# Starting the differential-attention steps four ticks earlier in a single-core hybrid attention layer

## The reference

```python
proj = h @ w_in                     # h: (512, 1024), w_in: (1024, 11264)
qa, ka, va, za, qd, kd, vd, zd, gm = split(proj)
# 24 windowed heads in three groups (dilation 1, 4, 16), each with its softmax denominator
o_g, lse_g = dilated_window_attention(rope(qa), rope(ka), va, ...)
alpha = softmax(stack(lses), axis=0)
ya = sum(alpha[..., None] * stack(outs)) * silu(za);  pa = ya @ w_proj_a
# 8 differential heads, two softmaxes each
qd, kd = rope(qd), rope(kd)
p = softmax(q_c @ k_c.T * 64 ** -0.5)        # c = 0, 1
yd = rms_norm((p[0] - lam * p[1]) @ vd, diff_subln) * 0.8 * silu(zd);  pb = yd @ w_proj_b
ga, gb = split(sigmoid(gm))
y = rms_norm((ga * pa + gb * pb) @ w_out, norm_post);  out = x + gate * y
```

## Time and profile before

| | |
|---|---|
| median of 3 runs | 801.05 us |
| range of these runs | 800.49 to 1100.22 us |
| the profiled execution | 801.21 us |
| its span | 799.1 us |
| PE busy | 778.6 us, 97% of the span |
| PE weight load busy | 656.9 us, 82% |
| DVE, ACT, POOL busy | 420.2, 359.9, 452.4 us |
| mean granted TensorE clock | 0.992 of full speed |

### The profile page before, as it was taken

How to read it: one execution, slowest core, us unless ns; L and a number is a source line. 1 busy time by engine, 2 the same in 40 slices (tenths; PEclk the granted TensorE clock), 3 DMA queues, 4 the chain that set the end, 5 groups by cost and what they waited for, 6 DMA issues and landing times.

```text
span 799.1 us, 12588 instructions
## 1 busy us (share of the span) xinstructions
PE 778.6 (97%) x4590; PEld 656.9 (82%) x4590; DVE 420.2 (53%) x692; ACT 359.9 (45%) x777; POOL 452.4 (57%) x577
## 2 busy tenths in 40 slices
PE   4999999999999999999999999999999999999997
PEld 3787898888888888898797888888787878878997
DVE  4766664635455443344675576487557445324432
ACT  5555535545444444343464555455556333314311
POOL 7854545446656654369663696596454287837200
PEclk9799999999999999999999999999999999999999
DMA  9955323233343432352431433242212145615431
GB/s 317 348 168 155 86 84 104 81 98 115 107 119 105 121 107 80 107 151 81 140 97 54 121 105 121 78 123 76 82 34 74 35 151 213 208 53 177 139 106 53
DMA packets 87075, 95.38 MB, mean 119 GB/s; under 512 B 9405, under 2 KB 78310, under 8 KB 87014
## 3 DMA queue, kind: packets, MB, share of 16 engines
q1 hardware_dynamic: 86944, 94.56, 38.3%
q10 hardware_dynamic: 70, 0.02, 0.0%
HBM read 78.53 MB, written 5.54 MB: 105 GB/s over the span
## 4 chain that ended last, share of the span: by engine, by line
PE 90%; issue 3%; POOL 3%; DVE 1%; DMA 1%; ACT 1%; SPq 0%; DVEq 0%; POOLq 0%; ACTq 0%
PE proj L1747 64%; PE sums L1670 4%; PE proj L1867 4%; PE score L1586 4%; PE turned L1638 3%; PE score L1620 3%; PE proj L1796 2%; PE sums L1672 2%; POOL w_lo L819 1%; PE score L1608 1%; DMA x_in<-in_x 1%; PE score L1796 1%; PE turned L1680 0%; PE turned L1694 0%; POOL merged L796 0%
## 5 line engine op out<-in xcount | busy, mean ns | idle before, releaser
L819 POOL TENSOR_TENSOR w_lo<-raw,w_hi 128x256 fp32r<-128x256 f32 x376 | 299.9, 829 | 212.7 <-ACT w_hi L932 212.7
L1747 PE MATMUL proj<-h_hi,w_hi 128*128 128x512 f32 x560 | 229.4, 410 | 0.1
L1747 PE MATMUL proj<-h_hi,w_lo 128*128 128x512 f32 x560 | 219.3, 392 | 0.0
L1747 PE MATMUL proj<-h_lo,w_hi 128*128 128x512 f32 x560 | 218.7, 391 | 0.0
L1747 PEld LDWEIGHTS proj<-h_hi,w_hi 128*128 128x128 f32 x560 | 105.2, 188 | 30.4 <-issue 9.6
L1747 PEld LDWEIGHTS proj<-h_hi,w_lo 128*128 128x128 f32 x560 | 105.1, 188 | 23.2
L1747 PEld LDWEIGHTS proj<-h_lo,w_hi 128*128 128x128 f32 x560 | 105.5, 188 | 19.1 <-issue 0.5
L932 ACT ACTIVATE w_hi<-raw 128x1024 fp32r<-128x1024 f32 x96 | 100.4, 1054 | 15.7 <-PE proj L1747 11.2
L1380 DVE TENSOR_TENSOR at_lo<-turned,at_hi 128x512 fp32r<-128x512 f32 x64 | 44.1, 689 | 80.6 <-ACT at_hi L1070 80.0
L848 POOL TENSOR_TENSOR rope_x<-rope_x,cos_t 128x512 f32<-128x512 f32 x36 | 53.4, 1484 | 51.6 <-DMA rope_s<-rope_x 51.6
L1670 PE MATMUL sums<-v,at_hi 128*128 128x128 f32 (+1 forms) x256 | 60.8, 307 | 0.0
(11 more groups left out here) (291 smaller groups left out, 1479.7 us busy)
## 6 DMA issues: line engine op xcount, KB each, us to landing
raw<-in_w_in SPq DMA_DIRECT2D x85, 512.0 KB, 3.6
rope_s<-rope_x SPq DMA_DIRECT2D x144, 64.0 KB, 2.0
ada<-in_w_ada SPq DMA_DIRECT2D x24, 256.0 KB, 7.1
raw<-in_w_proj_b SPq DMA_DIRECT2D x8, 512.0 KB, 3.4
zd<-in_w_ada SPq DMA_DIRECT2D x8, 512.0 KB, 4.6
raw<-in_w_out SPq DMA_DIRECT2D x8, 512.0 KB, 4.2
rows_in<-window_rows SPq DMA_DIRECT2D x4, 792.0 KB, 5.8
window_rows<-rows_out SPq DMA_DIRECT2D x4, 528.0 KB, 5.0
```

What stands on the lines that cost most here:

```text
L819: nc.gpsimd.tensor_tensor(lo[:, k, :], raw_place(n)[:, k, :], hi.bitcast(F32)[:, k, :], ALU.subtract).then_inc(w_lo_done, 1)
L1747: ins = mm(dst, left, right, start=k == 0 and n == 0, stop=k == nk - 1 and n == 2, skip_group_check=tile.b == 2)
```

## The change

Two lines change. The steps of stages 6 to 9 get a first tick of `t0[n + 1] - 4` in place of `t0[n + 1]`: the tick at which the zd block of their own stage begins, right behind its value block, in place of the tick at which the next stage (or `ga`) begins. So the steps of stage 6 go from ticks 96 to 110 to ticks 92 to 106, and those of stage 9 from 144 to 158 to 140 to 154. What is tied to a step (transposes, pv, head end, head turn) moves with it. The blends of row tiles 1, 2 and 3 go from ticks 116, 124 and 132 to 112, 120 and 128, with their loads, their work on POOL and their turns; that of tile 0 stays at tick 88, its turn at 96.

```diff
-        begin = t0[n + 1] + (0 if n else 2) + (g in (1, 2))
+        begin = t0[n + 1] - 4 if g == 3 else t0[n + 1] + (0 if n else 2) + (g in (1, 2))
...
-    mix_tick = [T0[6] + 16, T0[7] + 20, T0[7] + 28, T0[7] + 36]
+    mix_tick = [T0[6] + 16, T0[7] + 16, T0[7] + 24, T0[7] + 32]
```

## The result

The changed kernel takes **806.40 us** (median of 6 runs, 804.91 to 809.09), beside 801.15 us for the kernel before (6 runs, of which one slow run of 1100.22 us is left out of the ratio). The ratio is 1.0062, 95% interval 1.0047 to 1.0076: slower by 0.6%, within 2%. The forecast was 804.3, with a range from 801.5 to 808.0; rival (a), the forecast's stall with a clock that falls in it, stood at 806.8.

A forecast was written before the change was run, and what follows sets the result against it. PE was taken to bound the kernel, busy for 778.6 of 799.1 us. Terms of +4.45, -1.1 and -0.25 us, the others 0, gave +3.1 on 801.21: 804.3 us, range 801.5 to 808.0.

The forecast's parts named there:

- rival (a): Clock falls to half in the stage 6 gap, costing 0 to 5 us, taken 2.5: 806.8 us; chance 0.28.
- Part 1: First b tile: PE's wait for the last heads' low parts before the seventh and eighth slices goes, -1.1 us.
- Part 2: First scores of stage 6: PE stands still until the second k tile's low part is ready, +4.45 us.
- Part 3: zd block of stage 6: PE's wait for POOL's fourth w_lo slice is covered, -0.25 us.
- Part 4: First scores of stages 7, 8 and 9 at their earlier place: priced 0, upper bound +0.5 us.
- Part 5: Moved blends and head ends on POOL, DVE and SP: priced 0, bounds 0 and 0.5 us.
- Rival (b): No stall: k's swap in stage 6 lands in time and only gains stay, 799.9 us; chance 0.09.
- Rival (d): Joins come late at their new places over 32 steps, slower by over 2% (817.3 us); chance 0.02.

The follow-up runs named there:

- second profile: The changed kernel run once more, unaltered, and profiled again: 806.56 us, ratio 1.0058 to the kernel before.
- two-tick kernel: Changed kernel with the steps two ticks sooner in place of four, and blends 1 to 3 two ticks sooner: 809.73 us, ratio 1.0108.
- filler kernel: Changed kernel with 16 extra products of 128x512, their result overwritten, ahead of the wait for k at tick 92: 804.54 us, ratio 1.0053.
- swap-first kernel: Changed kernel with all blend loads one tick later on SP, tile 0's behind k's swap, blend work at its ticks: 808.37 us, ratio 1.0086.
- blends two ticks sooner: Changed kernel with steps and blends 1 to 3 two ticks sooner than the kernel before, heads' ends at their old ticks: 806.20 us, ratio 1.0046.

## Why the prediction was right, and where it was not

**Part 1 (wait for the last heads): right.** The distances in front of the seventh and eighth slices are usual again, and 1.09 us are gone. That the turn alone accounts for it is not so: putting it back costs 0.46 us in the trace. The rest goes with two operations of DVE that took 2.16 us beside POOL before and 1.47 us where POOL pauses.

**Part 2 (stall for k): right in mechanism and place, large by a tenth.** Forecast 4.45 us, measured 3.96 and, in the second profile, by the same distance 4.44 (listed as a wait of 4.3). The mechanism is shown from both sides: with blend 0 late the stall is gone, and the time with it; with the scores left where they were, moving blend 0 gains nothing that can be told. In the first profile the size was off because the swap landed 0.6 us sooner in relation to PE, less the 0.09 us by which the hand-over took 0.14 and not 0.05.

**Part 3 (slice of `w_lo`): right**, -0.25 us.

**Part 4 (first scores of stages 7 to 9): right** at 0, with 1.2 to 1.7 us to spare where the unaltered order would have been 0.2 late. The reason given, that blend turns and squares leave the value ticks, fits the two-tick kernel, in which the head's end entered the value ticks and PE waited seven times.

**Part 5 (blends and head ends): the price of 0 was wrong by 0.47 us**, just inside its bound of 0.5. Its step "the least cover that I found is 0.94 us" was read at one join of stage 8, a place without roundings of finished heads. At tick 151 a head's squares and a rounding meet in front of the same join, on ACT and DVE. The kernel with the roundings five ticks later shows that this is the cause of the wait.

**The step that failed is the choice between forecast and rival (a).** The prediction took a steady clock as the likelier (0.58 against 0.28), with the argument that "a fall right at the end of the idle time needs the unfavourable moment". The row it had, a fall 3.9 to 4.0 us after the last matmul, stood against a gap of 4.2 us: by its own numbers the fall was more likely than not, and the clock fell in both profiles that had this gap, once just ahead of the resumption and once just behind it. The Trainium skill (TensorE: Matmul & The Clock Gate, section "Why this matters for your kernels") warns of idle gaps of about this length; the traces agree, with a fall 3.9 us behind the last product, and show one behind a wait of 1.7 us as well. Rival (a)'s size was off the other way: it took half of 5 us, 2.5, for a low clock that lasted 3.4 us and cost 1.5. The filler kernel isolates this term: the same late k, full clock, 1.53 us less between the same products.

**The total.** Rival (a)'s 806.8 us is near 806.4, by errors that cancel: 0.5 us too much for the stall, 1.0 too much for the clock and 0.3 next to the waits stand against 0.5 too little for the join and 0.9 us that the landmarks behind the opening don't hold. That the sum came out within 0.4 us is luck. The forecast of +3.1 us is near the filler kernel's +3.7, which has the join's wait too. The prediction allowed for telling only 2%, 16 us, from no change; the interval is from 1.0047 to 1.0076, 2.3 us wide, and tells the forecast from rival (a).

**Rival (b)** fell, with the stall in both profiles. **Rival (d)** fell for this change, but its mechanism exists: in the two-tick kernel seven waits for head ends and turns cost 6.6 us. The price of a wrong tick was on record as 32 small waits, and it takes seven.

**What stays open:** in the kernel before with blend 0 late, the stretch behind the opening is 0.70 us shorter. Of that, 0.24 lies ahead of the value block of stage 6, and is scatter: this part takes 251.5 or 251.7 us in kernels of either kind. Of the remaining 0.46, the slice of `w_lo` is 0.35 (the 0.25, and 0.10 in the next distance). And the 0.9 us of the medians were not isolated: opening and clock are both candidates.

## What to carry to other kernels

Before an operation is moved ahead, look at what it reads and how late that was while nobody asked: the lateness of an input has no price in the old profile, and the whole of it is charged in the new one. Putting a queue right isn't enough when a second engine has the same two pieces of work in the same wrong order, as the swap-first kernel shows; move the work on all engines (the blend's tick) and not on one. Steps, head ends and blends that are placed at fixed distances hit other neighbours for each shift, so a smaller shift is not a smaller risk: two ticks cost 9 us, four ticks 5, and four ticks with blend 0 four ticks later as well cost nothing.

## What the runs showed of the hardware

**The clock can fall after less than 2 us of waiting.** With blends two ticks sooner, PE waited 1.7 us (525.64 + 0.39 to 527.70), and the granted clock went to 1.2 GHz at about 528.4, back at about 531.8. In the two-tick kernel none of the waits, of up to 1.6 us, touched it; across the longest the window reads:

```profile
488.00:489.00 1.00, 0.03 (x1) 1.00 0.14 45
```

In the swap-first kernel it fell 2.3 us after the last product, in the changed kernel 3.9. So the length of a gap alone doesn't tell whether it falls; behind the gap of 4 us it did in both profiles.

**DVE's scaling beside POOL.** All 32 scalings of each kernel from 90 us on, grouped (busy us, mean ns of one): the changed kernel, the kernel before and the two-tick kernel, each from its own trace.

```profile
L1423 DVE TENSOR_SCALAR head_sums<-head_sums,ystat 128x128 f32<-128x128 f32 x32 | 6.9, 279 | 1.9 <-POOL ystat L866 1.9
```

```profile
L1423 DVE TENSOR_SCALAR head_sums<-head_sums,ystat 128x128 f32<-128x128 f32 x32 | 8.5, 329 | 0.0
```

```profile
L1423 DVE TENSOR_SCALAR head_sums<-head_sums,ystat 128x128 f32<-128x128 f32 x32 | 21.2, 722 | 0.0
```

The same instruction takes from 0.87 us for four to 2.83 and 4.33 us, by what POOL does at the time. In the stretch of the two-tick kernel shown above, POOL's four slices at 0.8 us each and DVE's four at 0.7 us run side by side, as if each took turns. The Trainium skill (SBUF — State Buffer, section "Who interferes with whom") says that when DVE runs in a mode that uses two ports, which a `tensor_scalar` can, it and GpSimd exclude each other: whichever issues first holds the shared ports for its whole instruction. The rows agree in size, 0.71 us for one beside slices of 0.82, and no run here isolates the port.
